# Projection by quarters of the input columns in open banks; first conditioning product ahead of the fourth tile, later tiles normalised among the quarters

## The reference

```python
mod = jax.nn.silu(cond) @ w_ada + b_ada          # cond: c_ctx for the context, c for the latent tokens
sh1, sc1, g1, sh2, sc2, g2 = split(mod, 6)
h = modulate(rms_norm(x, norm_attn_g), sh1, sc1)  # xn * (1 + scale) + shift
q_g, k_g, v_g, g_g, lora, q_s, k_s, v_s = split_cols(h @ w_in)
```

## Time and profile before

| what | value |
|---|---|
| median of three runs | 1601.85 us |
| the profiled execution | 1599.84 us |
| its span, first to last instruction | 1598.0 us |
| TensorE busy | 1504.7 us, 94% |
| VectorE, ScalarE, GpSimd busy | 719.7, 530.2, 541.5 us |
| mean granted clock of TensorE | 0.973 |
| moved by the transfers | 301.66 MB, mean 189 GB/s |

### The profile page before, as it was taken

The page is one execution under the profiler, slowest core; times in us unless marked ns, Lnnn a source line. Parts: engine busy times, 40 slices in busy tenths (PEclk is TensorE's granted clock), DMA queues, the critical chain, the costliest instruction groups (busy, mean ns, idle before and its releaser), DMA issues. The chain is left out here.

```text
span 1598.0 us, 28991 instructions
## 1 busy us (share of the span) xinstructions
PE 1504.7 (94%) x9259; PEld 925.4 (58%) x9260; DVE 719.7 (45%) x1463; ACT 530.2 (33%) x1255; POOL 541.5 (34%) x605
## 2 busy tenths in 40 slices
PE   6999999999979999999899799999999999999977
PEld 2554678787847775555455455555555555555523
DVE  2400053333446662688753344444344444444438
ACT  2400066343056561211200034333333333333312
POOL 0001135333163311111055445455545555445410
PEclk8999999999979999999999899999999999999979
DMA  9991002010093108102000599999999999996589
GB/s 347 338 362 41 20 1 54 18 41 20 2 372 111 55 1 341 40 40 105 14 1 0 215 297 335 311 340 340 337 338 340 335 326 317 267 276 129 83 264 378
DMA packets 108677, 301.66 MB, mean 189 GB/s; under 512 B 13020, under 2 KB 24112, under 8 KB 107836
## 3 DMA queue, kind: packets, MB, share of 16 engines
q1 hardware_dynamic: 82686, 216.81, 35.9%
q0 software_dynamic: 25920, 83.91, 21.8%
HBM read 230.26 MB, written 80.90 MB: 195 GB/s over the span
## 5 line engine op out<-in xcount | busy, mean ns | idle before, releaser
L2186 PE MATMUL ps_g<-w_exp,mix 128*64 x1408 | 324.0, 383 | 6.7 <-DVE own_gu L2308 2.8
L2189 PE MATMUL ps_g<-own_gu,mix 128*64 128x256 f32 x1408 | 324.1, 383 | 0.0
L2133 POOL DMA_INDIRECT sum_rows<-mix,scatter_row x88 | 175.2, 1991 | 237.8 <-DVE mix L2245 219.0
L2186 PEld LDWEIGHTS ps_g<-w_exp,mix 128*64 128x64 f32 x1408 | 186.2, 137 | 107.2 <-issue 9.9
L2189 PEld LDWEIGHTS ps_g<-own_gu,mix 128*64 128x64 f32 x1408 | 186.2, 137 | 0.0
L2158 PE MATMUL ps_y<-w_exp,hidT 128*64 x352 | 171.6, 610 | 2.4 <-ACT own_d L2258 2.4
L2159 PE MATMUL ps_y<-own_d,hidT 128*64 128x512 f32 x352 | 171.6, 610 | 0.0
L511 PE MATMUL ps_f<-late,hT 128*128 128x256 f32 x624 | 145.3, 390 | 0.0
L2308 DVE COPY own_gu<-w_exp 128x2048 f32 x89 | 109.7, 1233 | 58.9 <-issue 43.6
L511 PEld LDWEIGHTS ps_f<-late,hT 128*128 128x128 f32 x624 | 120.2, 196 | 18.8 <-issue 1.9
L2245 DVE COPY mix<-ps_y 128x512 f32<-128x512 f32 x88 | 60.8, 691 | 112.8 <-PE ps_y L2159 112.8
(11 more groups left out here) (352 smaller groups left out, 2610.4 us busy)
## 6 DMA issues: line engine op xcount, KB each, us to landing
w_exp<-in_exp_w_gate SPq DMA_DIRECT2D x64, 512.0 KB, 5.9
w_exp<-in_exp_w_up SPq DMA_DIRECT2D x64, 512.0 KB, 6.7
w_exp<-in_exp_w_down SPq DMA_DIRECT2D x64, 512.0 KB, 7.5
sum_rows<-mix SPq DMA_DIRECT2D x10, 2048.0 KB, 18.4
w_exp<-sum_rows SPq DMA_DIRECT2D x36, 512.0 KB, 13.7
ada_ring<-in_w_ada SPq DMA_DIRECT2D x8, 2048.0 KB, 11.0
wring<-in_w_ada SPq DMA_DIRECT2D x3, 2048.0 KB, 13.0
h_rows<-h SPq DMA_DIRECT2D x9, 512.0 KB, 2.6
```

The costliest lines, as they stand in the source:

```text
L2133: pool.indirect_dma_start(out=dram["y"][k % 2], out_offset=bass.IndirectOffsetOnAxis(ap=si[k][:], axis=0), in_=y[k], in_offset=None, bound ...
L2186: pe.matmul(ps_g[par][0:HALF, 0:2 * FF].rearrange("p (k f) -> p k f", k=2), xT[par][:, j * P:j * P + HALF], w[:, bass.ds(slot * 3, 2), ff] ...
L2189: last = pe.matmul(ps_g[par][HALF:P, 0:2 * FF].rearrange("p (k f) -> p k f", k=2), xT[par][:, j * P + HALF:(j + 1) * P], own_gu[par][:, :, ...
```

## The change

SyncE loads four tiles first. Conditioning weights now come by quarters q of the input columns: quarter q holds columns 256q to 256q + 255 of shift and the same of scale (two loads of 1 MB), followed by the two row blocks 2q and 2q + 1 of the qk weights. Tiles 4 to 7, lora, gg, tile 8, the norm's constant and vg follow.

Tiles 0 to 3 are turned and copied to `hT` unmodulated (`low_plain`, `high_plain`). When quarter q's conditioning row is turned, VectorE makes four columns (`columns`) and scales row block 2q of these four tiles in place (`scale_even`), ScalarE row block 2q + 1 (`scale_odd`). TensorE then adds this row block's share to four open banks, one for each m (`part`, products over 512 tokens), with the next quarter's conditioning product and row between the parts. Tile 3 is turned behind the first conditioning product. Tiles 4, 5 and 6 are turned inside the third and fourth quarter, tiles 7 and 8 ahead of outputs 5 and 6, and they are modulated out of PSUM as before (`low_half`, `high_half`: four instructions each). The token groups of qk and lora become 512, 384 and 256. The bank for conditioning rows is one of its own; the banks of turned tiles are two of 512 columns, one for each half of a tile. ScalarE loads the table of roots at the start. The core of the diff:

```diff
+        NQ = 4
+        RAW = 4
+        GROUPS = [(0, 512), (512, 384), (896, 256)]
+        NB = 4
...
-        NX = 3
...
+        NX = 4
...
+        xin = [keep["mix"][:, NT * 512 + i * D:NT * 512 + (i + 1) * D] for i in range(NX - 1)] + [keep["mix"][:, 0:D]]
...
-        psT = ctx.enter_context(nc.psum_tensor("psT", [P, 2, D], F32))
-        NB = 3
+        psR = ctx.enter_context(nc.psum_tensor("psR", [P, 512], F32))
+        psT = ctx.enter_context(nc.psum_tensor("psT", [P, 2, 512], F32))
         psP = ctx.enter_context(nc.psum_tensor("psP", [P, NB, 512], F32))
...
+        ada_w = [slots[0][:], slots[1][:], slots[3], slots[0][:]]
+        qk_w, gg_w = slots[2][:], slots[1][:]
+        vg_w = [keep["late_half"](0), keep["late_half"](1)]
...
+            for t in range(RAW):
+                x_load(t)
+            for q in range(NQ):
+                if q == 3:
+                    sp.wait_ge(ada_done, 1)
+                for half in range(2):
+                    c0 = half * D + q * 256
+                    sp.dma_start(ada_w[q][:, :, half * 256:half * 256 + 256], w_ada[:, :, c0:c0 + 256]).then_inc(ada_in[q], 16)
+                sp.dma_start(qk_w[:, 2 * q:2 * q + 2, :], w_in[:, 2 * q:2 * q + 2, C_QK[0]:C_QK[0] + 512]).then_inc(qk_in[q], 16)
+            for t in range(RAW, NT - 1):
+                sp.wait_ge(xn_done, t - NX + 1)
+                x_load(t)
+            sp.dma_start(wlora[:], w_in[:, :, C_LORA[0]:C_LORA[0] + C_LORA[1]]).then_inc(lora_in, 16)
+            sp.wait_ge(ada_done, 2)
+            sp.dma_start(gg_w, w_in[:, :, C_GG[0]:C_GG[0] + C_GG[1]]).then_inc(gg_in, 16)
+            sp.wait_ge(xn_done, NT - NX)
+            x_load(NT - 1)
+            sp.dma_start(normg[:], dram["gla_norm_g"].to_broadcast([P, P])).then_inc(normg_in, 16)
+            sp.wait_ge(ada_done, 3)
+            for half in range(2):
+                c0 = C_VG[0] + half * 256
+                sp.dma_start(vg_w[half], w_in[:, :, c0:c0 + 256]).then_inc(vg_in[half], 16)
...
+            def xT(t):
+                pe.wait_ge(xn_done, t + 1)
+                for half, kept, turned in ((0, low_kept, low_turned), (1, high_kept, high_turned)):
+                    if t >= 1:
+                        pe.wait_ge(kept, t)
+                    for j in range(4):
+                        at = (4 * half + j) * P
+                        last = pe.transpose(psT[:, half, j * P:(j + 1) * P], xn[:, t % 2, at:at + P], keep["ident"][:])
+                    last.then_inc(turned, 1)
...
+            def part(j, m):
+                last = pe.matmul(psP[:, m, :], qk_w[:, j, m * P:m * P + P], hT[:, j, 0:512], start=(j == 0), stop=(j == KD - 1))
+                if j == KD - 1:
+                    last.then_inc(proj_done, 1)
+            for t in range(RAW - 1):
+                xT(t)
+            ada(0)
+            xT(RAW - 1)
+            turn_row(0)
+            for q in range(NQ):
+                pe.wait_ge(qk_in[q], 16)
+                pe.wait_ge(even_scaled, q + 1)
+                for m in range(4):
+                    part(2 * q, m)
+                pe.wait_ge(odd_scaled, q + 1)
+                if q + 1 < NQ:
+                    ada(q + 1)
+                    part(2 * q + 1, 0)
+                    part(2 * q + 1, 1)
+                    turn_row(q + 1)
+                    if q + 2 == NQ:
+                        xT(RAW)
+                    part(2 * q + 1, 2)
+                    part(2 * q + 1, 3)
+                else:
+                    for m in range(4):
+                        if m % 2 == 0:
+                            xT(RAW + 1 + m // 2)
+                        part(KD - 1, m)
+            def reuse(kk):
+                a = by_act(kk - NB)
+                pe.wait_ge(evac_act if a else evac_dve, evacs_before(kk - NB + 1, a))
+            for kk in range(4, len(outs)):
+                kind, m, t = outs[kk]
+                if kk in (5, 6):
+                    xT(kk + 2)
+                if kk == 4:
+                    pe.wait_ge(low_kept, 7)
+                    pe.wait_ge(high_kept, 7)
+                if kk == 8:
+                    pe.wait_ge(low_kept, NT)
+                    pe.wait_ge(high_kept, NT)
+                reuse(kk)
+                bank = source(kk)
...
+            def high_plain(t):
+                act.wait_ge(high_turned, t + 1)
+                act.activation(hT[:, 4:KD, t * P:(t + 1) * P], psT[:, 1, :].rearrange("p (j t) -> p j t", t=P),
+                               ACT.Copy).then_inc(high_kept, 1)
+            def scale_odd(q):
+                act.wait_ge(high_kept, RAW)
+                act.wait_ge(low_kept, RAW)
+                act.wait_ge(modA_done, q + 1)
+                j = 2 * q + 1
+                for c, cols in ((0, slice(0, P)), (1, slice(P, RAW * P))):
+                    last = act.activation(hT[:, j, cols], hT[:, j, cols], ACT.Identity,
+                                          scale=modA1[:, j, c:c + 1], bias=keep["mod"][:, j, c:c + 1])
+                last.then_inc(odd_scaled, 1)
...
+            square(0)
+            square(1)
+            high_plain(0)
+            square(2)
+            high_plain(1)
+            square(3)
+            high_plain(2)
+            high_plain(3)
+            for q in range(NQ):
+                if q == NQ - 1:
+                    for t in range(RAW, NT - 1):
+                        square(t)
+                scale_odd(q)
+            high_half(4)
+            high_half(5)
+            high_half(6)
+            evac(0)
+            evac(2)
+            high_half(7)
+            square(8)
+            high_half(8)
+            for k in range(4, len(outs)):
                 if by_act(k):
-                    act.wait_ge(proj_done, k + 1)
-                    act.activation(dest(kind, m, t), source(kind, k), ACT.Silu if kind == "gg" else ACT.Copy,
-                                   scale=scale_of(kind, m)).then_inc(evac_act, 1)
...
+            def low_plain(t):
+                dve.wait_ge(low_turned, t + 1)
+                dve.tensor_copy(hT[:, 0:4, t * P:(t + 1) * P],
+                                psT[:, 0, :].rearrange("p (j t) -> p j t", t=P)).then_inc(low_kept, 1)
...
+            def columns(q):
+                dve.wait_ge(row_turned, q + 1)
+                if q == 0:
+                    dve.wait_ge(vec_cols, 2)
+                at = slice(2 * q, 2 * q + 2)
+                bada = keep["vcol"][:, V_BADA:V_BADA + 16].rearrange("p (h j) -> p h j", h=2)[:, :, at]
+                dve.tensor_tensor(keep["mod"][:].rearrange("p (h j) k -> p h j k", h=2)[:, :, at, :],
+                                  modps[:, 4 * q:4 * q + 4, :].rearrange("p (h j) k -> p h j k", h=2),
+                                  bada.unsqueeze(3).to_broadcast([P, 2, 2, 2]), ALU.add).then_inc(mod_cols, 1)
+                dve.wait_ge(mod_cols, q + 1)
+                dve.scalar_tensor_tensor(out=modA1[:, at, :], in0=keep["mod"][:, 8 + 2 * q:10 + 2 * q, :], scalar=1.0,
+                                         in1=keep["vcol"][:, V_NA + 2 * q:V_NA + 2 * q + 2].unsqueeze(2).to_broadcast([P, 2, 2]),
+                                         op0=ALU.add, op1=ALU.mult).then_inc(modA_done, 1)
+            def scale_even(q):
+                if q == 0:
+                    dve.wait_ge(low_kept, RAW)
+                    dve.wait_ge(high_kept, RAW)
+                dve.wait_ge(modA_done, q + 1)
+                j = 2 * q
+                for c, cols in ((0, slice(0, P)), (1, slice(P, RAW * P))):
+                    last = dve.tensor_scalar(hT[:, j, cols], hT[:, j, cols], modA1[:, j, c:c + 1],
+                                             keep["mod"][:, j, c:c + 1], ALU.mult, ALU.add)
+                last.then_inc(even_scaled, 1)
...
             norm(0)
...
+            low_plain(0)
+            norm(2)
+            low_plain(1)
+            norm(3)
+            low_plain(2)
+            keep_row(0)
+            low_plain(3)
+            for q in range(NQ):
+                if q == NQ - 1:
+                    norm(4)
+                    norm(5)
+                if q >= 1:
+                    keep_row(q)
+                columns(q)
+                scale_even(q)
+            low_half(4)
+            norm(6)
+            low_half(5)
+            norm(7)
+            low_half(6)
+            evac(1)
+            evac(3)
+            low_half(7)
+            norm(8)
+            low_half(8)
+            for k in range(4, len(outs)):
                 if not by_act(k):
-                    dve.wait_ge(proj_done, k + 1)
-                    dve.tensor_scalar(dest(kind, m, t), source(kind, k), scale_of(kind, m), None,
```

More of the change, by code:

```diff
@@ L191, in ada @@
+            def ada(q):
+                pe.wait_ge(ada_in[q], 32)
+                if q == 0:
+                    pe.wait_ge(cond_done, 1)
+                else:
+                    pe.wait_ge(row_kept, q)
                 for j in range(KD):
                     strip = slice(32 * (j % 4), 32 * (j % 4) + 32)
[L193 to L194 removed]
```

(60 more changed lines are left out.)

155 lines of the change are left out of this document (30 added, 125 removed).

## The result

The changed kernel took 1585.11 us (median of four executions, 1585.02 to 1587.86) against 1601.93: ratio 0.9898, 95% interval 0.9882 to 0.9913. Both intervals exclude no change: 16.8 us faster in the first session (13.9 to 18.9 by the interval) and 15.4 in the second (11.2 to 15.7). Forecast were 10.1 us, and a range that ended at 1587.8.

A forecast was written before the change was run, and what follows sets the result against it. Loads to 35 us, then modulated tiles to 45, bound TensorE's start; 23.3 + 39.1 + 1.7 + 0.4 = 64.5, plus 122.9 ends the stage at 187.4, 10.1 earlier: 1601.85 - 10.1 = 1591.8 us, range 1587.8 to 1597.2.

The forecast's parts named there:

- rival A: Clock already high when the quarters begin: 13.1 us gained instead of 10.1, median 1588.8; chance 0.10.
- What bounds the kernel: Projection stage: loads bind to 35 us, modulated tiles to 45; from 45.16 TensorE never waits, 152.3 us of work.
- Loads: Conditioning weights arrive at 15.3, 22.0, 28.7 and 35.4 us; no wait for the later ones, 12 us slack at the end.
- Rival C: Loads bind, mixed rows moving at half the rate: gain gone, 1601.85 us; chance 0.05, including gain lost behind the stage.
- Ahead of the first part: Tiles, first conditioning product, row and scaling (0.6 us): first projection product at 23.3 us, 21.9 earlier than 45.16.
- TensorE's work: In the quarters: parts 27.5, conditioning products 5.7, rows 2.9, tiles 4 to 6 3.0; sum 39.1 us.
- Rival B: Narrow products in the quarters don't gain from the clock, 3.64 us each: 5.2 us more, 1597.0; chance 0.08.
- The wait for bank 0: At the second column group's start TensorE waits 0.4 us while ScalarE scales its half of tile 6, then empties the bank.
- The rest of the stage: Work left after the quarters end at 64.5 us: 122.9 us, so the stage ends at 187.4 against 197.5.
- The clock in the quarters: Low clock at first when the parts begin, costing 1.7 us; bounds nothing and 4.2 us.
- From the stage to the kernel: What the stage gains, the kernel gains: 10.1 us off the median 1601.85; the range allows 1.0 for later stages.
- Rival D: Open banks, changed at every product, make the clock fall repeatedly in the quarters: slower than before, 1608.5 us; chance 0.04.

The follow-up runs named there:

- before_later_by_2us: The kernel before, with 18 unused transposes of the identity behind its last projection product; 1605.53 us.
- turn_late: The changed kernel with tiles 0 to 2 turned behind the first conditioning product instead of ahead of it; 1597.30 us.
- no_quarters: The changed kernel with all four conditioning products and rows ahead of the first part, none between the parts; 1606.51 us.
- gaps_filled: The changed kernel with ten unused transposes in the wait ahead of tile 2 and one unused product ahead of the first part; 1587.47 us.
- look_b: The changed kernel, unaltered, executed once more for its profile; 1591.23 us.
- before_turning_early: The kernel before, with 32 unused transposes of the identity ahead of the first conditioning product; 1604.48 us.
- best: The changed kernel with 24 unused transposes ahead of tile 0 and bank 0 emptied ahead of ScalarE's half of tile 6; 1588.33 us.
- after: The changed kernel itself, first session, against the kernel before; 1585.11 us, ratio 0.9898.

## Why the prediction was wrong

The measured 1585.11 us lies 2.7 below the range. The fall of 16.7 us from 1601.85 is made up of 13.55 in the profiled stage, 1.3 behind it, and 1.9 because the profiled execution before was 2.0 cheaper than its median and the one after only 0.1. The lower end of the range, rival A's 13.1 and 1.0 for later stages, took in nearly all of the first two and nothing of the third: the prediction noted the 2.0 us and took them to stand after the change as well. Point by point:

*What bounds the kernel.* Right. Loads to 35 us, turned tiles to 45; the work behind it moved as a block. At 35.01 show no wait for the projection's weights; before_later_by_2us does, 1.76 us up to 35.24. The low stretches read from the earlier trace rows are nearer 1.6 and 4.2 us than 1.8 and 4.1 (means of 0.84 and 0.63 in their microseconds), which changes nothing in the 1.7 taken.

*Loads.* The first weights were forecast for 15.3 and arrived at 15.25 in turn_late; where else the product waited for them it started at 15.54 to 16.27. The later ones, seen where nothing else holds TensorE (no_quarters), came at 22.8, 29.5 and 36.8 instead of 22.0, 28.7 and 35.4. The rate of the changed kernel, in slices of 1.5 us to 60 us:

```profile
GB/s 0 101 297 399 396 395 369 350 349 359 371 347 349 349 360 380 388 385 387 394 386 349 348 354 391 412 407 407 273 360 385 388 404 348 387 387 376 406 411 410
```

It is at 347 to 371 GB/s from 9 to 22.5 us and again near 350 from 31.5 to 36, where the earlier trace rows had promised 391. The row length alone doesn't make that: from 12 to 13.5 us all 511 packets are under 2 KB, and the rate is 349; from 24 to 25.5 us all 569 are, and it is 388. What does is open. The slack hid it, and it was less than the 12 us forecast: the last conditioning weights came at 36.8 (no_quarters) and their product began at 44.41 in the changed kernel, 7.6 later. Rival C did not come.

*Ahead of the first part.* 23.3 forecast. The low course has 22.6 to 23.1, the high one 21.2 to 22.0. The scaling in place took 0.74 on VectorE (0.6 taken, 0.38 to 1.0 given) and 1.09 on ScalarE.

*TensorE's work.* The sum of 39.1 us fits: from 21.18 to 60.3 are 39.1. The conditioning products took 1.92 each (1.9 taken), the rows 0.95 (0.97). Rival B is out. The wait for bank 0 was 0.45 (0.4).

*The rest of the stage.* 122.9 forecast, 183.92 - 60.76 = 123.2 measured.

*The clock in the quarters: the step that failed first.* I took the low level at the start as the case, 1.7 us in the parts and about as much in front of them, and gave the high level (rival A) 0.10. The runs show it in five of nine executions. In the low course the forecast stage end of 187.4 is met by 186.91, 187.33 and 187.41; in the high one A's 13.1 us by 12.7 to 13.55. The prices of both levels were right, the chance was wrong: 1.7 us in the parts is what the low course pays (5.37 against 3.67), and the forecast of 187.4 came true only where the low level did. The trace before could not show which level the new sequence would get, and a level that no row settles wants a real chance for each side, not 0.73 to 0.10.

*From the stage to the kernel: the step that failed second.* The prediction says "what the stage gains, the kernel gains", subtracts the stage's gain of one profile from the median, and gives later stages 1 us in the range. The rest scatters with a standard deviation of 2.2 us. Of the 15.4 us between the medians (11 timed executions of the changed kernel: 1586.45; 1601.85 for the kernel before in that session), the stages account for some 13: the eight stage ends of the changed kernel average 185.5, the two of the kernel before 198.7. The four profiled rests of the unaltered changed kernel average 1398.4, 1.5 below the mean of all 18. That makes 14.7. Of the first four executions, median 1585.11, one is profiled, and it was on the cheap side of both (stage end 183.92, rest 1397.8); two others are within 0.1 us of it. That the kernel before is at 198.7 on average rests on two profiles only, and why the rests of the four are below the mean is not settled beyond scatter.

*Rival D,* the open banks as a cost to the clock, did not come. Once high, it stayed at 1.00 from 30 to 61 us in every profile of the changed kernel, with a bank change at every product and no wait of TensorE between 21.18 and 60.3 us. The passage of the Trainium skill ("TensorE: Matmul & The Clock Gate", section "A second HAM failure mode: psum-queue depth-cycling") lays the swinging clock to short idle times between groups of products, and those did not arise here. So the runs show that the change of bank by itself did not cost the clock; they don't test the passage for a kernel that does idle. The low stretches that there were lay before and in the first four parts and were over before 30 us. They lay behind waits, but the waits ahead of tile 2 and of the first part stand in the high courses too; that waits cause them was not shown (gaps_filled has one profile).

## What to carry to other kernels

When a product must wait for several loads, split the contraction, keep its outputs open in as many banks as it has output blocks, and compute what each quarter of the input needs between the parts: without that the gain was nil (1602.25 us). Prepare the input ahead of the first load as well: with the quarters alone 4.6 of the 15.4 us were left. Where the granted clock could be at either level at the start of a stretch, price both courses and give both a real chance; look at the same code in several profiles before taking one level as the case. When forecasting a small gain from one profile, first ask how that execution stands to the others, for here a second profile of the same code ended the changed stage 2.4 us later.

## What the runs showed of the hardware

- Executions of the same code differ by 2.2 to 3.5 us in one stage of 185, because the granted clock takes one of two courses (5 of 9 high, 4 of 9 low: stage ends 183.9 to 184.8 and 186.9 to 187.4); nothing lies between. What decides is open.
- A product with 32 stationary columns in four strips takes 3.64 us at the low clock and 1.92 at the high one, though the profile prints the clock as 1.00 for both (look_b from 16 to 19 us, where the product took 3.64; its first recorded change comes later). The duration of the product is the better witness there.
- Transposes in float32 count for the clock. With 32 of them ahead, the first product took 1.92 us (before_turning_early), without them 3.64 in both profiles of the kernel before; with 24 ahead, tiles 0 and 1 took 2.15 us and not 3.95 to 4.00 (best). In the kernel before, the clock rose from 0.50 to 1.00 between 39 and 40 us, where TensorE had done only transposes since 35.01.
- Weights in packets under 2 KB moved at 349 GB/s from 12 to 13.5 us and at 388 from 24 to 25.5 in one profile (after), so a rate taken from one stretch need not hold in another.
